# Two transformer-like blocks on one core: six gate slabs split in three passes and moved ahead, with the work around them reordered

## The chip, the cores and the metric

The kernel runs on 1 core of a Trainium2 chip. The metric is device time in microseconds (us) of one execution. TensorE (PE) multiplies, ScalarE (ACT) and VectorE (DVE) work elementwise, GpSimd (POOL) here only makes remainders of weights, and SyncE (SP) issues every transfer. A name such as `ps` is the one PSUM tensor of eight banks, which all engines but POOL read and write.

## The reference

The input is 256 tokens of width 1024. Two layers of `first_block` run, then one block of another kind. What matters is the first kind:

```
h = rms_norm(x, norm1_g);  z = h @ w_in
cq, ckv, kpe, gq, gk, gv, glr, gr, su, gates = split_in(z)
o_a = mla_mixer(cq, ckv, kpe, ...)        # low-rank attention, 8 heads
o_b = gla_mixer(gq, gk, gv, glr, gr, ...) # gated linear attention, chunks of 64
o_c = s5_mixer(su, lam_re, lam_im, ...)   # diagonal complex scan over time
g = sigmoid(gates + gate_b)               # 3 x 1024 gate columns
merged = g0*(o_a @ w_br_mla) + g1*(o_b @ w_br_gla) + g2*(o_c @ w_br_s5)
x = x + merged @ w_out
x = x + square(relu(rms_norm(x, norm2_g) @ w_ff1)) @ w_ff2
```

The last block projects queries, keys, values and gates, runs a dilated attention with a relative position bias, a convolution and its layer norm, a projection with a norm behind it, and a gated feed-forward part (tanh form of silu) with another norm behind it.

## The kernel before

Activations stand transposed, channels on partitions and the 256 tokens along the free axis. Weights come in slabs of 128x1024 numbers (512 KB), in the fixed order of `first_slabs`; a ring of three buffers holds raw slabs, and each split slab also has a rounded part `w_hi` (made by ACT) and a remainder `w_lo` (made by POOL from `raw` and `w_hi`). There are two ways to multiply by a slab. `product` uses the split form: three matmuls of type fp32r per 128 rows, 24 for a slab. `product32` uses the raw slab in full fp32: 8 matmuls for a slab, each of which the trace shows as two records. Before the change the 24 slabs of gate columns (`gates`) all use `product32` with the full-precision `hN`.

The order of each engine is written out by hand; counting semaphores hold it together, and nothing reorders it. In one layer TensorE does the 19 slabs of `Z`, four slabs of the values `gv`, then the small products for the S5 scan, four slabs `UQ`, two slabs `UKV`, and then a long stretch in which small products that depend on VectorE alternate with gate slabs. The names in this stretch are: `drive(h)` feeds step h of the S5 scan (its result is waited for as `bu_ps`), `outputs(h)` takes its states (`s_ok`); `head_sums` makes the squares' sums of q or k; `state_sums` makes the chunk states of the linear attention; `scores(n)` starts attention step n. VectorE's order there is: scale q (waits `qk_rs`, from ACT), `rotate_and_scan(2)` and `states(2)`, the masked copy into `Am` (raises `am_ok`), scale k, the running states `St` (raises `st_ok`), `rotate_and_scan(3)`, `y_take`, `states(3)`, the rotary parts of q in two halves, `rotate_and_scan(4)`, and the norm of the linear attention's output (raises `of_ok`, for which `scores(0)` waits). The decay of the scan (`lam_a`, `lam_s`) is computed at the head of a layer by some twenty tiny operations on VectorE and nine on ACT.

The diff touches `norm_rows`, `post_norm`, both feed-forward loops, `second_tables`, and the per-layer programs of ACT, DVE and PE.

Of the kernel before, what the change touches and what calls it, by code (L numbers as in the profile page):

```python
# [51 lines left out]
RING = 3  # L52

# [134 lines left out]
def build(nc, A, consts_dram, oneh_dram, where, out_dram, scratch):  # L188
# [21 lines left out]
    I_Z, I_GV, I_UQ, I_UKV, I_GATE = 0, 19, 23, 27, 29  # L210
# [18 lines left out]
    with ctx:  # L229
# [91 lines left out]
        Am = WK[:, 2560:3584].rearrange("p (h b c) -> p h b c", h=GH, b=NT)  # L321
        St = WK[:, 3584:4352].rearrange("p (n a e) -> p n a e", n=3, a=2)
# [3 lines left out]
        W4 = [[MD[:, 8192 + 512 * i:8704 + 512 * i].rearrange("p (j t) -> p j t", j=2) for i in range(4)],  # L326
# [96 lines left out]
        rot_ok = sig("rot_ok", 3)  # L423
        rot_rd = sig("rot_rd", 2)
# [101 lines left out]
        tab_z = sig("tab_z", 0)  # L526
# [30 lines left out]
        co_ok = sig("co_ok", 0)  # L557
        post_rs = sig("post_rs", 0)
# [34 lines left out]
        def norm_rows(act, A_, l, k, b, ready):  # L593
# [101 lines left out]
        def second_tables(sp):  # L695

            sp.dma_start(oneh, oneh_dram[:, 0:384]).then_inc(tab_in.s, 16)
            for g in range(3):
                sp.dma_start(tabl[33 * g:33 * g + 32, :], oneh_dram[33 * g:33 * g + 32, 384:408]).then_inc(tab_z.s, 16)
            for g in range(3):  # L700
                sp.dma_start(tabl[33 * g + 32:33 * g + 33, :], oneh_dram[33 * g + 32:33 * g + 33, 384:408])\
                    .then_inc(tab_in.s, 16)
            sp.dma_start(wdw, A["w_dw_2"][0]).then_inc(tab_in.s, 16)

        def second_bias(sp):

            for g in range(3):
                sp.dma_start(tabl[33 * g:33 * g + 32, 8 * g:8 * g + 8],
                             A["rel_bias_table_2"][:, 8 * g:8 * g + 8]).then_inc(tab_in.s, 16)
# [44 lines left out]
        def act_second(act):  # L754
# [47 lines left out]
            def post_norm(k, slab):  # L802

                act.preload_act_table_set("natural_log_exp_and_others")
                for b in range(NT):
                    if b == 0:
                        act.wait_ge(tm_out.s, tm_out(L, 3 * k - 1))
                    else:
                        act.wait_ge(used.s, used(L, slab + 1))
                    c = slice(16 + b, 17 + b)  # L810
                    link(A_(sqt[:, b, :], ps_half(k, b), ACT.Square, accum_out=nt[:, c]))
                    link(A_(nt[:, c], nt[:, c], ACT.Ln, scale=1.0 / DM, bias=C("eps4" if k == 1 else "eps")))
                    A_(nt[:, c], nt[:, c], ACT.Exp, scale=-0.5).then_inc(post_rs.s, 1)
                    if b == 0:
                        prep(slab + 3)
# [88 lines left out]
            for c in range(NC2):  # L904
                if c >= 2:
                    act.wait_ge(ff2_ok.s, c - 1)
                u = V_FF + 2 * c
                th, gt, up_ = ffb[c % 2]
                evacuate(u, up2_at(c) + 1, [(gt, pair(u % 3), ACT.Copy, {}),
                                            (th, pair(u % 3), ACT.Tanh, dict(scale=0.5))])  # L910
                evacuate(u + 1, up2_at(c) + 3, [(up_, pair((u + 1) % 3), ACT.Copy, {})])
# [3 lines left out]
        def dve_second(dve):  # L915
# [1512 lines left out]
```

## Time and profile before

| | before |
|---|---|
| median of 3 runs | 1540.09 us (1539.19 to 1540.39) |
| profiled execution, its own time | 1536.8 us |
| its span, first to last instruction | 1535.0 us |
| mean granted TensorE clock | 0.995 |
| busy: DVE, ACT, POOL | 58%, 45%, 58% of the span |
| split slabs of layers 1 and 2 (POOL L1283) | 206 |

The profile gives times of one execution. "Busy" of TensorE is counted with overlapping matmuls, so the cost of one is read from the distance between starts and not from its length. A row of the timeline is: start, length, engine, line, operation, output and inputs, shape, count; in brackets the idle time of that engine just before and who ended it. The first layer begins at 0, the second at about 505 us, the last block at about 1010 us.

### The profile page before, as it was taken

The numbers are of one execution on the slowest core, as the hardware profiler recorded it, in microseconds if no ns is written. First come the engines' busy times: TensorE is split into PE (matmuls) and PEld (weight loads), VectorE is DVE, ScalarE is ACT, GpSimd is POOL, SyncE is SP. The second block draws the span as 40 slices with busy tenths as digits, with TensorE's granted clock in tenths as the row PEclk, the third lists the DMA queues.
The fourth block names the chain that finished last, engine by engine and source line by source line (L and its number), as shares of the span: only waits on it lengthen the run. The fifth ranks groups of instructions, "written<-read, shape, count | busy, mean of one in ns | idle before, by whom it ended". The sixth has DMA issues, their size and how long they took to land.

```text
span 1535.0 us, 23998 instructions
## 1 busy us (share of the span) xinstructions
PE 1485.0 (97%) x9775; PEld 1317.3 (86%) x9775; DVE 889.6 (58%) x1407; ACT 698.4 (45%) x1052; POOL 882.8 (58%) x364
## 2 busy tenths in 40 slices
PE   7999999999999999999999999999999999899997
PEld 6977778889899897777788888989999988799996
DVE  5878875443433687886434455338993454265545
ACT  6544222554444654422255344464445655554443
POOL 4710000878888671000087788868885536688885
PEclk9999999999999999999999999999999999999999
DMA  6633344656666563333365577656664434456653
GB/s 187 162 107 78 96 106 123 193 153 188 183 185 187 150 174 87 94 96 100 124 194 162 173 218 218 190 152 186 180 188 124 135 104 124 137 177 183 190 179 124
DMA packets 321784, 234.47 MB, mean 153 GB/s; under 512 B 9676, under 2 KB 305131, under 8 KB 321674
## 3 DMA queue, kind: packets, MB, share of 16 engines
q1 hardware_dynamic: 321674, 232.94, 52.2%
q8 instruction: 77, 1.26, 0.4%
q14 instruction: 33, 0.27, 0.1%
HBM read 231.82 MB, written 1.09 MB: 152 GB/s over the span
## 4 chain that ended last, share of the span: by engine, by line
PE 84%; issue 5%; ACT 4%; POOL 4%; DVE 2%; DMA 1%; SPq 0%; POOLq 0%; DVEq 0%; ACTq 0%
PE ps L672 18%; PE ps L1943 14%; PE ps L1059 7%; PE ps L1060 7%; PE ps L1061 7%; PE ps L1926 6%; PE ps L1928 6%; PE ps L1927 6%; POOL w_lo L1283 4%; PE ps L1134 1%; PE ps L1171 1%; PE ps L2063 1%; PE ps L2077 1%; ACT w_hi L1317 1%; PE ps L2044 1%
## 5 line engine op out<-in xcount | busy, mean ns | idle before, releaser
L1283 POOL TENSOR_TENSOR w_lo<-raw,w_hi 128x1024 fp32r<-128x1024 f32 (+1 forms) x206 | 504.6, 2467 | 499.6 <-ACT w_hi L1317 497.2
L751 POOL TENSOR_TENSOR w_lo<-raw,w_hi 128x1024 fp32r<-128x1024 f32 x154 | 378.0, 2468 | 138.3 <-ACT w_hi L773 132.8
L1317 ACT ACTIVATE w_hi<-raw 128x1024 fp32r<-128x1024 f32 (+1 forms) x206 | 218.1, 1060 | 241.6 <-PE ps L672 75.8
L1059 PE MATMUL ps<-h_hi,w_hi 128*128 128x256 f32 x864 | 246.3, 285 | 1.8 <-DVE h_lo L928 1.3
L1060 PE MATMUL ps<-h_lo,w_hi 128*128 128x256 f32 x864 | 244.3, 283 | 0.0
L1061 PE MATMUL ps<-h_hi,w_lo 128*128 128x256 f32 x864 | 244.2, 283 | 0.0
L1926 PE MATMUL ps<-h_hi,w_hi 128*128 128x256 f32 (+1 forms) x816 | 233.3, 286 | 6.4 <-POOL w_lo L1283 4.3
L1927 PE MATMUL ps<-h_lo,w_hi 128*128 128x256 f32 (+1 forms) x816 | 231.3, 283 | 0.0
L1928 PE MATMUL ps<-h_hi,w_lo 128*128 128x256 f32 (+1 forms) x816 | 231.2, 283 | 0.0
L773 ACT ACTIVATE w_hi<-raw 128x1024 fp32r<-128x1024 f32 x154 | 162.0, 1059 | 116.2 <-PE ps L1061 43.3
L1943 PE MATMUL ps<-hN,raw 128*128 128x256 f32 x768 | 174.9, 383 | 0.0
L1059 PEld LDWEIGHTS ps<-h_hi,w_hi 128*128 128x128 f32 x864 | 165.5, 192 | 2.9 <-issue 2.4
L1943 PEld LDWEIGHTS ps<-hN,raw 128*128 128x128 f32 x768 | 143.0, 190 | 27.3 <-issue 9.1
L1060 PEld LDWEIGHTS ps<-h_lo,w_hi 128*128 128x128 f32 x864 | 165.6, 192 | 0.4
L1061 PEld LDWEIGHTS ps<-h_hi,w_lo 128*128 128x128 f32 x864 | 165.5, 192 | 0.0
L1926 PEld LDWEIGHTS ps<-h_hi,w_hi 128*128 128x128 f32 (+1 forms) x816 | 156.3, 192 | 9.9 <-POOL w_lo L1283 5.4
L1927 PEld LDWEIGHTS ps<-h_lo,w_hi 128*128 128x128 f32 (+1 forms) x816 | 156.5, 192 | 1.1
L1928 PEld LDWEIGHTS ps<-h_hi,w_lo 128*128 128x128 f32 (+1 forms) x816 | 156.4, 192 | 0.0
L1559 DVE TENSOR_TENSOR fr<-fr 128x512 f32<-128x512 f32 (+1 forms) x34 | 32.6, 960 | 199.6 <-ACT fr L1325 199.5
L672 PE MATMUL ps<-w_hi,c_hi 128*128 128x512 f32 x344 | 110.6, 400 | 5.3 <-POOL w_lo L1283 3.0
L672 PE MATMUL ps<-w_lo,c_hi 128*128 128x512 f32 x344 | 109.5, 396 | 0.0
L672 PE MATMUL ps<-w_hi,c_lo 128*128 128x512 f32 x344 | 109.5, 396 | 0.0
(325 smaller groups left out, 2523.6 us busy)
## 6 DMA issues: line engine op xcount, KB each, us to landing
raw<-in_w_in_dram SPq DMA_DIRECT2D x160, 512.0 KB, 3.8
raw<-in_w_ff_dram SPq DMA_DIRECT2D x128, 512.0 KB, 4.1
raw<-in_w_ffn_in_dram SPq DMA_DIRECT2D x44, 512.0 KB, 3.9
raw<-in_w_ffn_out_dram SPq DMA_DIRECT2D x22, 512.0 KB, 3.5
raw<-in_w_out_dram SPq DMA_DIRECT2D x16, 512.0 KB, 3.4
raw<-in_w_br_gla_dram SPq DMA_DIRECT2D x8, 512.0 KB, 3.5
raw<-in_w_br_mla_dram SPq DMA_DIRECT2D x8, 512.0 KB, 3.6
raw<-in_w_br_s_dram SPq DMA_DIRECT2D x8, 512.0 KB, 4.0
```

The source lines that it names most:

```text
L672: last = MM(out(2 * b + h), x[:, k, tb], y[:, 512 * h:512 * h + 512], start=first_k and n == 0, stop=last_k and n == 2, skip_group_check=True)
L751: nc.gpsimd.tensor_tensor(out=w_lo[(NS * L + i) % RING][:, 0:kt * n], in0=raw[(NS * L + i) % RING][:, 0:kt * n], in1=w_hi[(NS * L + i) % R ...
L773: A_(w_hi[(NS * L + i) % RING][:, 0:kt * n], raw[(NS * L + i) % RING][:, 0:kt * n], ACT.Copy).then_inc(hi_done.s, 1)
L1059: MM(out, w[0], x[0], start=first_k, stop=False, skip_group_check=skip)
L1060: MM(out, w[0], x[1], start=False, stop=False, skip_group_check=skip)
L1061: return MM(out, w[1], x[0], start=False, stop=last_k, skip_group_check=skip)
L1283: nc.gpsimd.tensor_tensor(out=w_lo[(NS * l + i) % RING][:, 0:kt * n], in0=raw[(NS * l + i) % RING][:, 0:kt * n], in1=w_hi[(NS * l + i) % R ...
L1317: A_(w_hi[(NS * l + i) % RING][:, 0:kt * n], raw[(NS * l + i) % RING][:, 0:kt * n], ACT.Copy)\
L1926: a = MM(out, w[0], x[0], start=first_k, stop=False, skip_group_check=skip)
L1927: MM(out, w[0], x[1], start=False, stop=False, skip_group_check=skip)
L1928: return MM(out, w[1], x[0], start=False, stop=last_k, skip_group_check=skip)
L1943: last = MM(out, w[:, k, c0:c0 + n], x[:, x0 + k, :], start=k == 0, stop=k == kt - 1)
```

## The change

The gate slabs 0 to 5 of each layer are now split slabs: they are multiplied by `product` with `h_hi` and `h_lo`, and stand in the slab order behind the four `gv` slabs, ahead of `UQ`. The S5 transposes of B stand behind `Z` slab 16, those of C and the product of `glr` behind `Z` slab 18, `drive(0)` behind two `gv` slabs, `drive(1)` between the early gate slabs, `outputs(0)` and `drive(2)` between the `UKV` slabs. The decay's VectorE part stands ahead of `norm_lo` in layer 1 and behind it in layer 2 (before: behind `norm_h` in both), and its ACT part ahead of the first evacuation of `Z`. Scratch memory changes place (`Am` and `St` to `MD`, one set of scan buffers to `WK`). The feed-forward products write their DVE intermediates into PSUM, the norm behind a projection multiplies by its weight first and in PSUM, the first norm row block is squared in one operation, and the bias tables of the last block come as one array in one transfer.

```diff
+GATES_Z = 6
...
+    gates = [(0, KD, C_GATE + P * gate_tile(i), P) for i in range(24)]
+    s += [("w_in_z", *g) for g in gates[:GATES_Z]]
     s += [("mla_w_uq", 0, 3, 2 * QK * i, 2 * QK) for i in range(4)]
     s += [("mla_w_ukv", 0, 2, 512 * i, 512) for i in range(2)]
-    s += [("w_in", 0, KD, C_GATE + P * gate_tile(i), P) for i in range(24)]
+    s += [("w_in", *g) for g in gates[GATES_Z:]]
...
+                        if i < GATES_Z:
+                            last = product(l, gate_slab(i), out, 0, P, h_hi, h_lo)
+                        else:
+                            last = product32(l, gate_slab(i), out, 0, P, hN)
...
+                if l == 0:
+                    decay()
                 norm_lo(dve, stt, l, col, "norm1_g")
+                if l:
+                    decay()
...
+                gates(0, 4)
+                pe.wait_ge(bu_rd.s, bu_rd(l, 1))
+                drive(1)
+                gates(4, 6)
                 for s in range(4):
                     i = I_UQ + s
...
                 head_sums(qsq, U_QS)
-                outputs(0)
-                gates(0, 2)
-                pe.wait_ge(bu_rd.s, bu_rd(l, 2))
-                drive(2)
+                gates(6, 8)
+                outputs(1)
                 pe.wait_ge(qkt_ok.s, qkt_ok(l, 1))
+                pe.wait_ge(kr_ok.s, kr_ok(l, 1))
...
                 last.then_inc(a_ps.s, 1)
-                gates(2, 4)
...
                 state_sums(2, PO, 256)
-                outputs(1)
                 pe.wait_ge(bu_rd.s, bu_rd(l, 3))
                 drive(3)
                 pe.wait_ge(am_ok.s, am_ok(l, 1))
                 state_sums(1, PA[2], 0).then_inc(ds_ps.s, 1)
-                gates(4, 6)
                 pe.wait_ge(st_ok.s, st_ok(l, 1))
...
                 rotate_q(0)
-                gates(6, 7)
+                gates(8, 9)
                 pe.wait_ge(rot_rd.s, rot_rd(l, 1))
                 rotate_q(1)
-                gates(7, 8)
...
-                    gates(8 + b, 9 + b)
-                gates(10, 11)
+                    gates(9 + b, 10 + b)
...
-                    link(tt(f, f, f, ALU.mult))
-                    link(V.tensor_copy(f_hi[c % 2][:, :, :], f))
-                    split_lo(f_lo[c % 2][:, :, :], f, f_hi[c % 2][:, :, :]).then_inc(ff_sq.s, 1)
+                    link(tt(x, fr[:, c % 2, :, :], x, ALU.mult))
+                    link(V.tensor_copy(f_hi[c % 2][:, :, :], x))
+                    split_lo(f_lo[c % 2][:, :, :], x, f_hi[c % 2][:, :, :]).then_inc(ff_sq.s, 1)
...
+            if b == 0:
+                act.wait_ge(*ready(1))
+                A_(sqt[:, 0, :], xt[:, 0, :], ACT.Square, accum_out=c[2]).then_inc(norm_sq.s, 2)
...
-            sp.dma_start(oneh, oneh_dram[:, 0:384]).then_inc(tab_in.s, 16)
-            for g in range(3):
-                sp.dma_start(tabl[33 * g:33 * g + 32, :], oneh_dram[33 * g:33 * g + 32, 384:408]).then_inc(tab_z.s, 16)
...
+            sp.dma_start(PT2[0][0:99, 0:408], A["bias_tables"]).then_inc(tab_in.s, 16)
...
-                link(stt(gt, th, 1.0, gt, ALU.add, ALU.mult))
-                link(tt(gt, gt, up_, ALU.mult))
+                link(stt(gt, th, 1.0, gate, ALU.add, ALU.mult))
+                dve.wait_ge(used.s, used(L, up2_at(c) + 4))
+                link(tt(up_, gt, up_, ALU.mult))
```

First place, TensorE in the middle of a layer. Before, from the third step of the scan's drive to the linear attention's output (`L1943` are gate slabs, eight matmuls each; `L2063` is `drive`, `L2077` `outputs`, `L2044` `head_sums`, `L2156` `state_sums`, `L2175` the output that waits for `st_ok`):

```order
L2063 MATMUL ps<-Z,BT 128x256 x4
L2137 MATMUL ps<-cst,WK 128x128 x4
L2044 MATMUL ps<-G,cst 96x512 x4
L2146 MATMUL ps<-WK 128x128 x8
L1943 MATMUL ps<-hN,raw 128x256 x16
L2156 MATMUL ps<-gv,WK 64x128 x8
L2077 MATMUL ps<-Z,CT 32x256 x4
L2063 MATMUL ps<-Z,BT 128x256 x4
L2156 MATMUL ps<-gv,WK 64x128 x4
L1943 MATMUL ps<-hN,raw 128x256 x16
L2175 MATMUL ps<-WK,gv 128x128 x2
```

Two pairs of gate slabs stand in this stretch, and one more directly ahead of it, behind the head sums of q. The same place now, from the head sums of q on (`L1965` gate slabs, `L2034` `drive`, `L2121` `outputs`, `L2106` `head_sums`, `L2188` `state_sums`, `L2205` the output that waits for `st_ok`):

```order
L2106 MATMUL ps<-MD,cst 96x512 x4
L1965 MATMUL ps<-hN,raw 128x256 x16
L2121 MATMUL ps<-Z,CT 32x256 x4
L2170 MATMUL ps<-cst,WK 128x128 x4
L2106 MATMUL ps<-G,cst 96x512 x4
L2179 MATMUL ps<-WK 128x128 x8
L2188 MATMUL ps<-gv,WK 64x128 x8
L2034 MATMUL ps<-Z,BT 128x256 x4
L2188 MATMUL ps<-gv,WK 64x128 x4
L2205 MATMUL ps<-MD,gv 128x128 x2
```

One pair of gate slabs is left between the head sums of q and the linear attention's output, where three pairs stood; no gate slab stands behind the head sums of k any more.

Second place, VectorE at the head of the first layer. Before (`L1562` is `norm_lo`, `L616` `norm_h`, the rest the decay):

```order
L1562 SCALAR_TENSOR_TENSOR h_lo<-ps,cols,h_hi 128x256 x8
L616 TENSOR_SCALAR hN<-ps,cols 128x256 x8
L1597 TENSOR_SCALAR sms<-cols 128x16
L1559 TENSOR_TENSOR ps<-sms,ps 128x16
L1559 TENSOR_TENSOR ps<-cols,ps 128x16
L1600 TENSOR_SCALAR ps<-ps 128x16
L1601 CAST smi<-ps 128x16
L1602 CAST sms<-smi 128x16
```

And now:

```order
L1611 TENSOR_SCALAR sms<-cols 128x16
L1576 TENSOR_TENSOR ps<-sms,ps 128x16
L1576 TENSOR_TENSOR ps<-cols,ps 128x16
L1614 TENSOR_SCALAR ps<-ps 128x16
L1615 CAST smi<-ps 128x16
L1616 CAST sms<-smi 128x16
L1579 SCALAR_TENSOR_TENSOR ps<-sms,ps 128x16 x3
L1619 TENSOR_SCALAR ps<-ps 128x16
L1579 SCALAR_TENSOR_TENSOR h_lo<-ps,cols,h_hi 128x256 x8
```

The decay's first part stands ahead of `h_lo`, for which the first slab's matmuls wait.

Third place, ACT at the head of a layer. Before (`L1335` is `h_hi`, `L1317` a slab's `w_hi`, `L1325` an evacuation of `Z`, the rest the decay):

```order
L1335 ACTIVATE h_hi<-ps,cols 128x256 x8
L1317 ACTIVATE w_hi<-raw 128x1024 x2
L1325 ACTIVATE Z<-ps 128x512
L1317 ACTIVATE w_hi<-raw 128x1024 x2
L1325 ACTIVATE Z<-ps 128x512
L1368 ACTIVATE sms<-ps 128x16
```

And now:

```order
L1350 ACTIVATE h_hi<-ps,cols 128x256 x8
L1332 ACTIVATE w_hi<-raw 128x1024
L1370 ACTIVATE sms<-ps 128x16
L1371 ACTIVATE ps<-ps 128x16
L1372 ACTIVATE ps<-sms 128x16
L1374 ACTIVATE sms<-cols 128x16
```

The decay on ACT stands three slabs earlier: `w_hi` of slabs 3 to 5 is made behind it instead of ahead of it.

## Rows read from the trace of the kernel before

**Rows 1.** The page's part 1: busy time, share and instructions.

```profile
PE 1485.0 (97%) x9775; PEld 1317.3 (86%) x9775; DVE 889.6 (58%) x1407; ACT 698.4 (45%) x1052; POOL 882.8 (58%) x364
```

**Rows 2.** The page's part 4: shares of the chain that ended last.

```profile
PE 84%; issue 5%; ACT 4%; POOL 4%; DVE 2%; DMA 1%; SPq 0%; POOLq 0%; DVEq 0%; ACTq 0%
```

**Rows 3.** Timeline of PE, 24 matmuls of a split slab apart.

```profile
26.82 0.28 PE L1926 MATMUL ps<-h_hi,w_hi 128*128 128x256 f32 x1
...
29.70 0.28 PE L1926 MATMUL ps<-h_hi,w_hi 128*128 128x256 f32 x1
```

**Rows 4.** Timeline of PE, middle of the first layer.

```profile
118.70 3.82 PE L2044 MATMUL ps<-MD,cst 96*96 96x512 f32 x8
...
123.44 7.17 PE L1943 MATMUL ps<-hN,raw 128*128 128x256 f32 x32
130.54 1.14 PE L2063 MATMUL ps<-Z,BT 32*128 32x256 f32 x8
...
185.64 0.71 PE L2222 MATMUL ps<-MD 96*128 96x128 f32 x4
```

**Rows 5.** Timeline of ACT, the exponential that releases q's scaling.

```profile
123.28 1.91 ACT L1446 ACTIVATE MD<-MD 96x2048 f32<-96x2048 f32 x1
```

**Rows 6.** Timeline of DVE, the same stretch of the first layer.

```profile
125.22 2.35 DVE L1562 SCALAR_TENSOR_TENSOR MD<-MD,cols 96x2048 f32<-96x2048 f32 x1 [0.86 <-ACT MD L1446]
131.80 2.48 DVE L1559 TENSOR_TENSOR MD<-ps,AR 128x512 f32<-128x512 f32 x4 [4.23 <-PE ps L2063]
...
141.98 1.33 DVE L1762 COPY_PREDICATED WK<-cst,ps 128x512 f32<-128x512 int32 x2
...
149.61 2.48 DVE L1559 TENSOR_TENSOR Z<-ps,AR 128x512 f32<-128x512 f32 x4
...
161.01 1.22 DVE L1559 TENSOR_TENSOR MD<-ps,cst 32x1024 f32<-32x1024 f32 x1 [0.75 <-PE ps L2187]
...
166.50 1.22 DVE L1559 TENSOR_TENSOR MD<-ps,cst 32x1024 f32<-32x1024 f32 x1 [1.76 <-PE ps L2187]
...
180.04 1.22 DVE L1562 SCALAR_TENSOR_TENSOR MD<-sq,MD 128x1024 f32<-128x1024 f32 x1
...
186.46 0.43 DVE L1559 TENSOR_TENSOR ps<-ps,cst 128x256 f32<-128x256 f32 x1 [0.94 <-PE ps L2222]
```

**Rows 7.** Timeline of PE, the wait in the first slabs of each layer.

```profile
36.68 0.48 PE L1926 MATMUL ps<-h_hi,w_hi 128*128 128x256 f32 x1 [2.13 <-POOL w_lo L1283]
...
532.95 0.39 PE L1926 MATMUL ps<-h_hi,w_hi 128*128 128x256 f32 x1 [2.13 <-POOL w_lo L1283]
```

**Rows 8.** Table of stretches: PE, PEld, DVE, ACT, POOL busy, clock, DMA.

```profile
36.00:42.00 6.00, 5.32 (x32) 5.32 (x33) 5.32 (x18) 1.16 (x2) 5.29 (x3) 0.72 0.58 152
```

**Rows 9.** Timelines of POOL, DVE and ACT at the heads of the layers.

```profile
15.10 2.37 POOL L1283 TENSOR_TENSOR w_lo<-raw,w_hi 128x1024 fp32r<-128x1024 f32 x1 [2.28 <-ACT w_hi L1317]
...
24.69 2.40 POOL L1283 TENSOR_TENSOR w_lo<-raw,w_hi 128x1024 fp32r<-128x1024 f32 x1 [0.80 <-ACT w_hi L1317]
...
24.80 2.31 DVE L1602 CAST sms<-smi 128x16 f32<-128x16 int32 x1
...
515.26 4.80 POOL L1283 TENSOR_TENSOR w_lo<-raw,w_hi 128x1024 fp32r<-128x1024 f32 x2 [1.51 <-ACT w_hi L1317]
...
525.59 0.18 ACT L1368 ACTIVATE sms<-ps 128x16 f32<-128x16 f32 x1
...
528.11 1.28 ACT L1378 ACT_TABLE_LOAD   x1
```

**Rows 10.** Timelines of PE and DVE: transfers' wait, last block's end.

```profile
859.76 1.22 PE L672 MATMUL ps<-w_hi,c_hi 128*128 128x512 f32 x2 [2.53 <-POOL w_lo L1283]
...
1522.04 0.74 PE L672 MATMUL ps<-w_hi,c_hi 128*128 128x512 f32 x2 [2.30 <-DVE c_lo L928]
...
1529.67 0.76 DVE L928 SCALAR_TENSOR_TENSOR ps<-ps,nt,Up 128x512 f32<-128x512 f32 x1
...
1531.86 0.69 DVE L925 TENSOR_TENSOR xt<-xt,ps 128x512 f32<-128x512 f32 x1
```

More of the change, by code:

```diff
@@ L804, in post_norm @@
                 act.preload_act_table_set("natural_log_exp_and_others")
+                n = 4 * (k - 1)
                 for b in range(NT):
[L806 to L813, printed above, removed]
+                    rs_, part = nt[:, 16 + b:17 + b], nt[:, 18 + b:19 + b]
+                    for i in (2 * b, 2 * b + 1):
+                        if i < 3:
+                            act.wait_ge(tm_out.s, tm_out(L, 3 * (k - 1) + i + 1))
+                        else:
+                            act.wait_ge(used.s, used(L, slab + 1))
+                        y = ps_out(i) if k == 1 else ps_tok(i)
+                        A_(tok(sqt, i), y, ACT.Square, accum_out=rs_ if i % 2 else part).then_inc(post_sq.s, 1)
+                        if i % 2 == 0:
+                            act.wait_ge(post_sq.s, n + i + 1)
+                            link(A_(part, part, ACT.Identity, scale=1.0 / DM, bias=C("eps4" if k == 1 else "eps")))
+                    act.wait_ge(post_sq.s, n + 2 * b + 2)
+                    link(A_(rs_, rs_, ACT.Ln, scale=1.0 / DM, bias=part))
+                    A_(rs_, rs_, ACT.Exp, scale=-0.5).then_inc(post_rs.s, 1)
                     if b == 0:
@@ L907, in act_second @@
                 u = V_FF + 2 * c
[L908 to L911, printed above, removed]
+                th = ffb[c % 2][0]
+                evacuate(u, up2_at(c) + 1, [(th, pair(u % 3), ACT.Tanh, dict(scale=0.5))])
+                prep(up2_at(c) + 3 + RING)
             prep(N2)
@@ L1423, in _ @@
                 A_(e1[:, :, :], e1[:, :, :], ACT.Ln, bias=C("one")).then_inc(gg_ex.s, 1)
-                for u in range(4):
-                    b = pair((U_UQ + u) % PGF)[0:QK]
-                    evacuate(U_UQ + u, I_UQ + u, [
-                        (q[0:QK, 2 * u:2 * u + 2, :], b, ACT.Copy, {}),
-                        (qsq[0:QK, 2 * u:2 * u + 2, :], b, ACT.Square, {})])
+                take_gv(1)
+                gate(0)
                 act.wait_ge(cs_ok.s, cs_ok(l, 1))
@@ L1437, in _ @@
                     .then_inc(ge_ok.s, 1)
+                gate(1)
+                gate(2)
+                for u in range(4):
+                    b = pair((U_UQ + u) % PGF)[0:QK]
+                    evacuate(U_UQ + u, I_UQ + u, [
+                        (q[0:QK, 2 * u:2 * u + 2, :], b, ACT.Copy, {}),
+                        (qsq[0:QK, 2 * u:2 * u + 2, :], b, ACT.Square, {})])
                 def head_rms(k, dst, U):
@@ L2001, in _, with drive @@
                 x_to_h(pe, l, 0, 1)
+                def drive(h):
+                    g, j0 = h // 2, 2 * (h % 2)
+                    for jj in range(2):
+                        rr_ = slice(32 * (j0 + jj), 32 * (j0 + jj) + 32)
+                        for r in range(2):
+                            last = MM(pair(4 + jj)[:, r, :], BT[rr_, r, g, :], Z[rr_, Z_SU + g, :],
+                                      start=True, stop=True)
+                    last.then_inc(bu_ps.s, 1)
                 pe.wait_ge(consts_all.s, 16)
```

273 lines of the change are left out of this document (140 added, 133 removed).

## The prediction

> **What bounds the kernel now.** I read the page's busy table first: TensorE is busy 97% of the span and VectorE 58% [rows 1]. The chain that ended last runs 84% through TensorE [rows 2]. So a microsecond taken from TensorE's own work is won, a microsecond in which it waits is lost, and VectorE and POOL count only where one of them arrives last. Shares of the whole span hide the one thing that matters for this change: in the middle of each layer there is a stretch in which VectorE is nearly full. I read it next, in the timelines of TensorE and VectorE. Call T the end of the head sums of q, at 118.70 + 3.82 = 122.5 [rows 4]. From there TensorE reaches `scores(0)` at 185.6, that is T+63.1 [rows 4]. VectorE finishes what `scores(0)` waits for at 180.04 + 1.22 = 181.3, T+58.7 [rows 6]. In between it idles only 4.23, 0.75 and 1.76, each time for TensorE, 6.7 in all; its 0.86 ahead of the scaling of q is for ACT's exponential, which ends at 125.19 [rows 5, 6]. TensorE therefore is not waiting in this stretch, but only because gate slabs fill it. Last I read the waits: 2.13 early in each layer [rows 7], and 2.53 and 2.30 in the last block [rows 10].
>
> **The slabs' price.** A split slab takes from 26.82 to 29.70, 2.88 us [rows 3]. An unsplit pair takes from 123.44 to 130.54, 7.10, so 3.55 for one [rows 4]. Twelve slabs change form: 12 x 0.67 = -8.0 us. ACT makes twelve more `w_hi` and POOL twelve more `w_lo` of some 2.4 us each [rows 9]; POOL is at 58% and idle where they fall, so I cost these at nothing; without that cover they are the second rival.
>
> **The gap in the middle of a layer.** This is the term that decides. Six gate slabs, three pairs, leave the part behind T and lie ahead of it now: 3 x 7.10 = 21.3 less work for TensorE behind T. It takes one `outputs` and one `drive` off it as well, of eight records each, 1.0 and 1.1 by the row of 1.14 [rows 4]. Together 23.4, so TensorE's own work from T to `scores(0)` falls from 63.1 to 39.7. All that VectorE has to do from T stays, in the same order: scale q, step 2 of the scan, the copy to `Am`, scale k, the running states, step 3, the rotary halves, step 4, the norm of the output. That queue is 58.7 long with its 6.7 of idle, and 52.0 without. `drive(2)` being early removes the 4.23, and I take all three as removed. The second rotary half can't be: TensorE sends `rotate_q(1)` only when VectorE has read the first, for which I leave 0.7. So `scores(0)` starts at T+52.7, and TensorE idles 52.7 - 39.7 = about 13; I take 12.9. By the trace, 23.4 is taken away, 4.4 of it was slack of TensorE over VectorE and 6.7 of VectorE over TensorE, and the rest must show as waits. They spread: the first at the state sums for `am_ok` (the copy at 141.98 follows scan step 2 [rows 6]), the larger at `st_ok`, which has the scaling of k and the running states ahead of it, and the last at `outputs(2)` and `scores(0)` for `of_ok`. Behind the waiting matmul stands TensorE's whole queue, among it the products that VectorE needs next, so the wait can't be used for other slabs. Bounds: nothing lost (0), if VectorE had 13 us more in reserve than its idle rows show; 16.7 lost, if its idle stays for lack of anything sent early. I stay at 12.9, near which the rows of idle time are.
>
> **What is late next.** Behind `scores(0)` VectorE still has the second part of step 4, from 181.3 to 185.5 (it next idles 0.94 up to 186.46) [rows 6]. Before, this lay beside the 4.4 of slack. Now it stands ahead of the first softmax, and TensorE has a gate slab of 3.55 to cover 4.3 plus the first softmax row: I take +1.5, between 0 and 4.3. Small things in the same layers: waits for B and for the transposed values go, a bank is freed later by the evacuation of `gv`, and the remainders of the early gate slabs come only a few tenths ahead; I net these at -0.4, between -1.5 and +2.
>
> Per layer 12.9 + 1.5 - 0.4 = 14.0; two layers +28.0, with the slabs' price +20.0.
>
> **Heads of the layers.** In layer 1 the wait of 2.13 at 36.68 goes, because ACT's decay no longer stands ahead of a `w_hi`, and with it the lower clock behind it: the stretch 36 to 42 has 0.72 granted [rows 7, 8], which I price at 1.5. Against that, nine operations stand ahead of `h_lo` on VectorE. By the rows they are short, but the copy of 16 columns `sms<-smi` lasted 2.31, from 24.80 to 27.11, while POOL worked from 24.69 to 27.09 [rows 9]: it ended when POOL's operation ended. At its new place POOL's operation of 15.10 to 17.47 covers it [rows 9], so I give the first slab 2.2 of delay. Net -1.4; bounds -3.6 and +1. The Trainium skill ("SBUF — State Buffer", Who interferes with whom) says that VectorE and GpSimd share one port pair as an exclusive lock, held for a whole instruction by whoever started first; a cast is among the operations that can want it. The trace agrees with its 2.31; without that rule one would give the small operations some 0.2 each and the net would be -3.0.
>
> In layer 2 the decay stands behind `norm_lo` and ahead of the full-precision `hN`. Its first operations meet POOL's two remainders, 515.26 to 520.06, of which the first ends at 517.7 [rows 9]. `lam_a` then comes at about 519.7, ACT's decay lasts 2.5 (525.59 to 528.11) [rows 9], the next `w_hi` is ready at 523.3 and its remainder 2.4 later at 525.7. TensorE wants that slab at about 522.0: a wait of 3.7, less the 2.13 at 532.95 [rows 7], +1.6. Bounds -2 and +4.
>
> **The last block.** The bias tables come in one transfer in place of several; the wait of 2.53 at 859.76 for a remainder whose slab queued behind them goes [rows 10], with about 1.2 of slower clock behind it: -3.7, between 0 and -4. The feed-forward's last `c_lo` no longer waits behind VectorE's copies with two inputs in SBUF: -2.3 of 1522.04 [rows 10]. At the very end four pairs of 0.76 and 0.69 [rows 10] stand between the last norm and the output; the multiply by the weight now lies ahead of the norm's scale, so that less of each pair stands behind it: -1.9, two thirds of the four 0.76, between 0 and -3. Other norms of this kind -0.5. Squaring the first row block in one operation begins later but is shorter, +0.1 at each of four norms: +0.5. Together -4.2, and with the transfers -7.9.
>
> **Sum.** +20.0 - 1.4 + 1.6 - 7.9 = +12.3. The profiled execution took 1536.8, of which the span is 1535.0; it becomes 1549.1. The median of the runs is 1540.09, 3.3 above the profiled one, 0.2%: a difference of executions that the change does not touch. So 1552.4.
>
> **Rivals.** *The stretch does not bind.* If VectorE catches up, what is left is the slabs' price, the small items, the heads and the last block: -8.0 - 0.8 + 0.2 - 7.9 = -16.5, 1523.6. It needs `of_ok` at T+40 in place of T+52. For it speaks that VectorE gets 21 us of TensorE's work ahead of T in which to run ahead; against it, that the scaling of q stands first in its queue behind T and ACT's exponential releases that only at T+2.7 [rows 5], and that the 52 is time in which it was working. It decides from 12 us of VectorE's queue done ahead of T; the new order moves only the drive of step 2, not the step. Chance 0.08.
>
> *The remainders fall behind as well.* In the ten slabs from the first of `gv` to gate slab 5, TensorE uses one each 2.88 while POOL needs 2.4, and in the same time VectorE runs multiplies with both inputs in SBUF, of 1.2 and more, as the 1.22 in the output's norm [rows 6]. If each of these takes a turn with POOL, a slab costs 2.4 + 1.2 = 3.6 and six slabs lose 0.7 each, 4 per layer, and a lower clock behind the waits some more: +21 to +26 in all, 1561 to 1566. For it speaks the copy of 2.31; against it, that at 58% POOL holds its pace in the `Z` slabs, with no wait but 2.13. Chance 0.13. By the same rule of the Trainium skill (same page and section) every VectorE operation with two SBUF inputs contends with a POOL operation that reads SBUF, which would make this the rule and not the exception; no row here shows six of them in such a run.
>
> *Half of it hides.* If VectorE's operations are shorter in the new stretch, because POOL has less to do beside them, a layer loses 7 in place of 14: 1538, no change. Chance 0.07.
>
> **How the numbers follow.** Forecast 0.72, rivals 0.08, 0.13 and 0.07. The forecast's own spread is 2 per layer in the gap and some 3 in the rest: 1546 to 1559. For 8 in 10 I take 1544 to 1560, which takes in part of the port's case; fast and half-hidden cases stay outside. Within 0.2% means 3.1 us, about what a measurement can tell. Faster: 0.08 and a little of the third case, 0.09. Same: 0.05. Slower: 0.86.
>
> **What would show it.** Right: in each layer TensorE idles some 13 us between T and `scores(0)`, released by VectorE (`Am`, `St`, output norm), and VectorE has no idle time above 1 us there except for ACT's exponential. The early gate slabs start 2.88 apart. The waits of 2.53 and 2.30 are gone; in layer 2 a remainder of an early `Z` slab is late by 3 to 4. Wrong: the waits at the state sums are under 3 us together (then T's own position hides something that I missed), or gate slabs 0 to 5 start 3.5 apart (then POOL is the bound), or the granted clock falls for long after the new gaps.

## The result, and the profile after

| | before | changed |
|---|---|---|
| median | 1540.24 us (1539.19 to 1540.39) | 1554.87 us (1552.25 to 1559.43) |
| ratio | | 1.0100, 95% interval 1.0075 to 1.0124 |
| span of the profiled execution | 1535.0 us | 1553.1 us |
| mean granted clock | 0.995 | 0.984 |

The change makes the kernel 1.0% slower, 14.6 us by the medians; 1552.4 was forecast. The two profiled spans are 18.1 apart, because the profiled execution of before (1536.8) lay 3.4 under its median and that of the changed kernel on its own. The page's part 1 of the changed kernel, to be held against [rows 1]:

```profile
PE 1485.6 (96%) x9871; PEld 1323.3 (85%) x9871; DVE 759.8 (49%) x1407; ACT 696.5 (45%) x1036; POOL 893.6 (58%) x376
```

TensorE's busy time is the same although 12 slabs became shorter, and VectorE has 130 us less of busy time while the kernel is slower. The chain of waits shows what took TensorE's place (part 4, against [rows 2]):

```profile
PE 80%; DVE 7%; issue 4%; ACT 4%; POOL 3%; DMA 1%; SPq 0%; DVEq 0%; POOLq 0%; ACTq 0%
```

VectorE had 2% of the chain and has 7%. The timeline of TensorE shows where, in the first layer; T, the end of q's head sums, is 135.35 + 3.82 = 139.2 here (against [rows 4]):

```profile
135.35 3.82 PE L2106 MATMUL ps<-MD,cst 96*96 96x512 f32 x8
139.12 7.14 PE L1965 MATMUL ps<-hN,raw 128*128 128x256 f32 x32
...
155.90 0.65 PE L2188 MATMUL ps<-gv,WK 64*64 64x128 f32 x8 [1.29 <-DVE MD L1784]
162.28 1.22 PE L2205 MATMUL ps<-MD,gv 128*128 128x128 f32 x4 [5.73 <-DVE MD L1579]
...
179.84 1.14 PE L2034 MATMUL ps<-Z,BT 32*128 32x256 f32 x8 [0.26 <-DVE MD L1576]
...
192.84 0.68 PE L2250 MATMUL ps<-MD 96*128 96x128 f32 x4 [1.65 <-DVE MD L1579]
```

`scores(0)` starts at T+53.7, where T+63.1 was before. In between TensorE waits four times, 8.9 us in all, each time for VectorE. The remaining 44.7 are still 5.0 more than the 39.7 of work. The table of stretches shows where (columns as in [rows 8]):

```profile
156.00:162.00 6.00, 0.55 (x8) 0.31 (x8) 5.85 (x7) 1.74 (x2) 0.00 (x0) 0.70 0.00 0
162.00:170.00 8.00, 7.72 (x40) 6.47 (x40) 7.89 (x14) 0.00 (x0) 0.00 (x0) 0.50 0.00 0
170.00:174.00 4.00, 4.00 (x21) 1.80 (x20) 3.65 (x6) 1.02 (x1) 0.00 (x0) 0.74 0.00 0
```

TensorE worked 0.55 of the 6 us up to 162, and the clock granted from 162 to 170 is 0.50, the 1.2 GHz level. The products behind the wait ran at half speed: from the first of them to the first gate slab behind them it is 10.7 us (162.28 to 172.97), where before it was 6.2 (154.66 to 160.90). That is 4.5 of the 5.0. VectorE meanwhile is 5.85 of 6.00 and 7.89 of 8.00 busy. Its timeline, against [rows 6]:

```profile
141.94 2.35 DVE L1579 SCALAR_TENSOR_TENSOR MD<-MD,cols 96x2048 f32<-96x2048 f32 x1 [15.01 <-ACT MD L1466]
144.32 2.48 DVE L1576 TENSOR_TENSOR WK<-ps,AR 128x512 f32<-128x512 f32 x4
...
154.51 1.33 DVE L1784 COPY_PREDICATED MD<-cst,ps 128x512 f32<-128x512 int32 x2
...
162.14 2.48 DVE L1576 TENSOR_TENSOR Z<-ps,AR 128x512 f32<-128x512 f32 x4
...
173.07 1.22 DVE L1576 TENSOR_TENSOR MD<-ps,cst 32x1024 f32<-32x1024 f32 x1 [0.28 <-PE ps L2217]
...
178.56 1.22 DVE L1576 TENSOR_TENSOR MD<-ps,cst 32x1024 f32<-32x1024 f32 x1 [1.76 <-PE ps L2217]
...
191.47 1.23 DVE L1579 SCALAR_TENSOR_TENSOR MD<-sq,MD 128x1024 f32<-128x1024 f32 x1
```

The idle 4.23 is gone, 0.75 became 0.28, 1.76 stayed, and VectorE ends this queue at 192.7, T+53.5. Ahead of the scaling of q VectorE sits idle for 15.0 us: that is what the six slabs bought, idle time for the engine that is late behind T. In layer 2 the same waits stand at the same distances (1.28, 5.73, 0.26, 1.65).

The distance between the two kernels, by the start of the same operation in both, splits the total:

| up to | before | changed | distance | this part | forecast |
|---|---|---|---|---|---|
| T, layer 1 | 122.5 | 139.2 | +16.7 | +16.7 | +18.0 |
| `scores(0)`, layer 1 | 185.6 | 192.8 | +7.2 | -9.5 | -10.4 |
| second norm, layer 1 | 323.0 | 332.6 | +9.6 | +2.4 | +1.1 |
| second norm, layer 2 | 817.2 | 839.9 | +22.7 | +13.1 | +11.6 |
| last block's first slab | 1014.7 | 1036.3 | +21.6 | -1.1 | -3.7 |
| end | 1535.0 | 1553.1 | +18.1 | -3.5 | -4.2 |

(The +18.0 is six slabs of 2.88 and the 2.1 of one `outputs` and one `drive`, less 1.4 at the head; -10.4 is T+52.7 less T+63.1.) The stretch with the bias table is off by most, 2.6; layer 2 comes next with 1.5. Of a single row not more than some 1.5 us can be read: up to the product `ps<-sq,cst` behind the first twelve slabs of layer 1, the changed kernel took 54.8 us, and the run with the decay moved in layer 2 (below), which has the same code there, took 56.1.

The places of the smaller terms in the changed kernel, TensorE's timeline, against [rows 7] and [rows 10]:

```profile
18.78 0.55 PE L1948 MATMUL ps<-h_hi,w_hi 128*128 128x256 f32 x1 [3.63 <-DVE h_lo L1579]
...
93.14 0.28 PE L1948 MATMUL ps<-h_hi,w_hi 128*128 128x256 f32 x1
...
96.02 0.28 PE L1948 MATMUL ps<-h_hi,w_hi 128*128 128x256 f32 x1
...
289.90 0.35 PE L1948 MATMUL ps<-o_hi,w_hi 128*128 128x256 f32 x1 [2.21 <-POOL w_lo L1298]
...
535.27 0.58 PE L1948 MATMUL ps<-h_hi,w_hi 128*128 128x256 f32 x1 [3.43 <-POOL w_lo L1298]
...
881.94 1.17 PE L688 MATMUL ps<-w_hi,c_hi 128*128 128x512 f32 x2 [2.00 <-POOL w_lo L1298]
```

The two rows at 93 and 96 are the first products of two early gate slabs, 2.88 apart. The cast that [rows 9] have at 2.31 is here, in layer 1 and in layer 2:

```profile
14.86 2.14 DVE L1616 CAST sms<-smi 128x16 f32<-128x16 int32 x1
...
528.22 0.17 DVE L1616 CAST sms<-smi 128x16 f32<-128x16 int32 x1
```

And two stretches of the table (columns as in [rows 8]), the one behind the wait of 3.43 and the one ahead of the wait of 2.00:

```profile
535.00:541.00 6.00, 5.73 (x28) 5.73 (x29) 5.34 (x14) 0.36 (x2) 4.90 (x3) 0.53 0.69 176
...
879.40:881.00 1.60, 0.54 (x3) 0.10 (x1) 1.01 (x2) 1.43 (x3) 1.48 (x1) 1.00 0.07 20
```

In the second, the DMA engines are busy for 0.07 on average, which is about one of sixteen, and move 20 GB/s.

### The profile page after: what moved, and what is told of

Read it like the earlier page. It is cut to its first block, busy times and chain, and to the rows that moved or that the text cites. A ratio compares the mean times of both kernels' runs of the same rounds, so it can differ in the third digit from the quotient of the medians.

```text
span 1553.1 us, 24229 instructions
## 1 busy us (share of the span) xinstructions
PE 1485.6 (96%) x9871; PEld 1323.3 (85%) x9871; DVE 759.8 (49%) x1407; ACT 696.5 (45%) x1036; POOL 893.6 (58%) x376
## 3 DMA queue, kind: packets, MB, share of 16 engines
q8 instruction: 78, 1.28, 0.3%
## 4 chain that ended last, share of the span: by engine, by line
PE 80%; DVE 7%; issue 4%; ACT 4%; POOL 3%; DMA 1%; SPq 0%; DVEq 0%; POOLq 0%; ACTq 0%
PE ps L688 17%; PE ps L1965 10%; PE ps L1948 7%; PE ps L1949 7%; PE ps L1950 7%; PE ps L1074 6%; PE ps L1075 6%; PE ps L1076 6%; POOL w_lo L1298 2%; DVE WK L1576 2%; PE ps L1149 1%; DVE MD L1579 1%; PE ps L1186 1%; DMA raw<-in_w_ff_dram 1%; ACT w_hi L1332 1%
## 5 line engine op out<-in xcount | busy, mean ns | idle before, releaser
L1298 POOL TENSOR_TENSOR w_lo<-raw,w_hi 128x1024 fp32r<-128x1024 f32 x218 | 521.7, 2404 | 503.8 <-ACT w_hi L1332 502.7
L756 POOL TENSOR_TENSOR w_lo<-raw,w_hi 128x1024 fp32r<-128x1024 f32 x154 | 371.6, 2421 | 144.8 <-ACT w_hi L778 143.4
L1332 ACT ACTIVATE w_hi<-raw 128x1024 fp32r<-128x1024 f32 x218 | 230.1, 1058 | 242.5 <-PE ps L688 91.3
L1948 PE MATMUL ps<-h_hi,w_hi 128*128 128x256 f32 (+1 forms) x912 | 261.9, 287 | 9.2 <-DVE h_lo L1579 5.7
L1949 PE MATMUL ps<-h_lo,w_hi 128*128 128x256 f32 (+1 forms) x912 | 259.4, 284 | 0.0
L1950 PE MATMUL ps<-h_hi,w_lo 128*128 128x256 f32 (+1 forms) x912 | 259.3, 284 | 0.0
L778 ACT ACTIVATE w_hi<-raw 128x1024 fp32r<-128x1024 f32 x154 | 161.7, 1057 | 142.0 <-PE ps L1076 76.0
L1948 PEld LDWEIGHTS ps<-h_hi,w_hi 128*128 128x128 f32 (+1 forms) x912 | 175.9, 193 | 13.0 <-issue 7.7
L1949 PEld LDWEIGHTS ps<-h_lo,w_hi 128*128 128x128 f32 (+1 forms) x912 | 176.0, 193 | 1.2
L1576 DVE TENSOR_TENSOR ps<-fr,ps 128x512 f32<-128x512 f32 (+1 forms) x36 | 24.0, 666 | 269.5 <-ACT fr L1340 258.0
L1965 PE MATMUL ps<-hN,raw 128*128 128x256 f32 x576 | 131.8, 383 | 0.0
L1965 PEld LDWEIGHTS ps<-hN,raw 128*128 128x128 f32 x576 | 107.0, 190 | 21.1 <-issue 7.7
```

Source lines behind the costliest of these rows:

```text
L756: nc.gpsimd.tensor_tensor(out=w_lo[(NS * L + i) % RING][:, 0:kt * n], in0=raw[(NS * L + i) % RING][:, 0:kt * n], in1=w_hi[(NS * L + i) % R ...
L778: A_(w_hi[(NS * L + i) % RING][:, 0:kt * n], raw[(NS * L + i) % RING][:, 0:kt * n], ACT.Copy).then_inc(hi_done.s, 1)
L1298: nc.gpsimd.tensor_tensor(out=w_lo[(NS * l + i) % RING][:, 0:kt * n], in0=raw[(NS * l + i) % RING][:, 0:kt * n], in1=w_hi[(NS * l + i) % R ...
L1332: A_(w_hi[(NS * l + i) % RING][:, 0:kt * n], raw[(NS * l + i) % RING][:, 0:kt * n], ACT.Copy)\
L1948: a = MM(out, w[0], x[0], start=first_k, stop=False, skip_group_check=skip)
L1949: MM(out, w[0], x[1], start=False, stop=False, skip_group_check=skip)
```

## The experiments

The kernel before ran beside each group, with medians of 1537.9, 1538.4 and 1538.8. Differences against the changed kernel are taken between the ratios, times 1540. Its own ratio is known to 0.0025, which is 3.8 us, so a smaller difference rests on the traces and not on the medians. T and `scores(0)` come from each run's timeline.

### Is the gap VectorE's queue?

Put gate work back behind T. `GATES_Z` becomes 4, and the two pairs stand unsplit behind T; the run with 2 puts three pairs there.

```diff
-GATES_Z = 6
+GATES_Z = 4
...
-                gates(4, 6)
                 for s in range(4):
                     i = I_UQ + s
...
                 head_sums(qsq, U_QS)
-                gates(6, 8)
+                gates(4, 6)
...
                 state_sums(1, PA[2], 0).then_inc(ds_ps.s, 1)
+                gates(6, 8)
                 pe.wait_ge(st_ok.s, st_ok(l, 1))
```

> Four gate slabs early in place of six: the pair 4,5 is unsplit again and stands behind the head sums of q, and the pair 6,7 stands ahead of the wait for the running states, where the kernel before had a pair. Theory (VectorE's queue behind T sets the start of scores(0), T being the end of q's head sums): scores(0) stays at T+53.6, T comes 2 x 2.88 = 5.8 earlier, the wait for St (5.73) goes to nearly nothing; -5.8 per layer, -11.5 in all, 1543. Rival (the gap is not VectorE's queue; a slab put there only adds its own time): the two unsplit slabs cost 0.67 more each, +2.7, 1557.5.

Measured: 1542.56, ratio 1.0026 (1.0011 to 1.0040), 11.4 under the changed kernel. T is 133.8 and `scores(0)` 185.91, T+52.1. TensorE's timeline:

```profile
150.52 0.65 PE L2187 MATMUL ps<-gv,WK 64*64 64x128 f32 x8 [1.28 <-DVE MD L1784]
...
185.91 0.95 PE L2250 MATMUL ps<-MD 96*128 96x128 f32 x4 [1.65 <-DVE MD L1579]
```

The wait of 5.73 is gone, and 7.1 us of work was put behind T while `scores(0)` even came a little earlier relative to T. The rival's +2.7 is out.

> Two gate slabs early in place of six: pairs 2,3, 4,5 and 6,7 stand unsplit at the three places of the kernel before; everything else of the change stays. Theory: TensorE's work between T and scores(0) is 39.7 + 14.2 = 53.9, equal to VectorE's 53.6, T comes 4 x 2.88 = 11.5 earlier, scores(0) at T+54 to T+56; -10 to -11.5 per layer, -21 in all, 1534, below the kernel before. Rival as in the run with four: +5.3, 1560.

Measured: 1537.53, ratio 0.9994 (0.9984 to 1.0004), 16.3 under the changed kernel and equal to before. T is 128.1, and `scores(0)` comes at T+56.2:

```profile
184.29 0.68 PE L2251 MATMUL ps<-MD 96*128 96x128 f32 x4 [1.64 <-DVE MD L1579]
```

The first pair put back gave 11.4 and the second only 4.9: TensorE's own 53.9 (39.7 and two pairs of 7.1) is nearly VectorE's time now. The size, -21, was too large, by 2.3 per layer of T+56.2 over T+53.9.

### Is it the length of the queue or the order of its operands?

Step 2 of the scan goes into the 15.0 us of idle time.

```diff
                 tt(kpe_r[NOPE:QK], kpe_r[NOPE:QK], kpe_g[NOPE:QK], ALU.add).then_inc(kr_ok.s, 1)
+                rotate_and_scan(2)
+                states(2)
...
                 dve.wait_ge(qk_n.s, qk_n(l, 2))
-                rotate_and_scan(2)
-                states(2)
```

> VectorE does step 2 of the scan (10.2 us) ahead of the scaling of q, in its idle time of 15.0 us. Theory A (every operation behind T waits for its own releaser, and the copy to Am and k's scaling wait for TensorE's products and for ACT): VectorE then idles for the A matrix (T+13.4) and for k's factors (T+15), St comes 1.4 earlier; -1.4 to -2 per layer, 1551 to 1552. Theory B (only the length of VectorE's queue counts): -9 per layer, 1537.

Measured: 1553.26, ratio 1.0095 (1.0080 to 1.0110), 0.8 under the changed kernel, with an interval that holds no difference. Theory B, -9 per layer, is out. Theory A fits the trace: T is 139.8 and `scores(0)` starts at 191.7, T+51.8, 1.8 earlier than in the changed kernel; the medians do not confirm its size. VectorE's timeline shows 8.3 of the 10.2 us come back as idle time:

```profile
142.61 2.35 DVE L1579 SCALAR_TENSOR_TENSOR MD<-MD,cols 96x2048 f32<-96x2048 f32 x1 [0.41 <-ACT MD L1466]
153.24 1.36 DVE L1783 COPY_PREDICATED MD<-cst,ps 128x512 f32<-128x512 int32 x2 [8.28 <-PE ps L2178]
```

The matrix A stands on TensorE behind a gate pair and k's head sums. The next run takes the pair away from there.

```diff
                 head_sums(qsq, U_QS)
-                gates(6, 8)
                 outputs(1)
...
                 drive(3)
+                gates(6, 8)
                 pe.wait_ge(am_ok.s, am_ok(l, 1))
                 state_sums(1, PA[2], 0).then_inc(ds_ps.s, 1)
```

> As the run with step 2 early, and TensorE does k's head sums, the A matrix, two state sums and drive(3) ahead of gate pair 6,7 instead of behind it. Theory A: VectorE's operands now come at T+6 and T+9, its queue ends at T+45 to T+47 in place of T+53.6, the wait for St goes; -6 to -8 per layer, -14 in all, 1541. Theory B: as the run before, 1537. If neither the operands nor the queue bind: 1551 to 1555.

Measured: 1546.13, ratio 1.0055 (1.0036 to 1.0073), 6.9 under the changed kernel, half of what was expected. VectorE's timeline names the other half:

```profile
147.09 1.35 DVE L1783 COPY_PREDICATED MD<-cst,ps 128x512 f32<-128x512 int32 x2 [1.76 <-PE ps L2177]
...
156.87 0.42 DVE L1795 COPY MD<-ps 128x256 f32<-128x256 f32 x1 [3.58 <-PE ps L2186]
...
175.85 1.22 DVE L1576 TENSOR_TENSOR MD<-ps,cst 32x1024 f32<-32x1024 f32 x1 [2.79 <-PE ps L2216]
```

I had put the pair ahead of the last state sum, for which `St` waits 3.58. `scores(0)` starts at T+49.9, where T+45 to T+47 was expected. Neither theory gave the size: queue length and operand order bind together.

### The smaller terms

The slab's price: the early slabs unsplit, in the same order.

```diff
-    s += [("w_in_z", *g) for g in gates[:GATES_Z]]
+    s += [("w_in", *g) for g in gates[:GATES_Z]]
...
-                            last = product(l, gate_slab(i), out, 0, P, h_hi, h_lo)
+                            last = product32(l, gate_slab(i), out, 0, P, hN)
```

> The six early gate slabs stay where the change put them but are multiplied unsplit (hN and the raw slab). Theory (a slab's price is 3.55 against 2.88, and POOL's and ACT's work for the split is hidden): T comes 6 x 0.67 = 4.0 later in each layer, nothing else moves, +8.0, 1563. Rival (the remainders of the early slabs hold TensorE or VectorE back, through the port that POOL and VectorE share): less than +4, under 1559.

Measured: 1561.39, ratio 1.0149 (1.0129 to 1.0169), 7.5 above the changed kernel. T comes 3.5 later, and the waits for VectorE behind it are the same 1.29, 5.73 and 1.64. The price of -8.0 fits, within the intervals of some 4 us, and the trace shows no wait up to `scores(0)` that the split adds.

The bias table: only the convolution's weights are moved.

```diff
             sp.dma_start(PT2[0][0:99, 0:408], A["bias_tables"]).then_inc(tab_in.s, 16)
-            sp.dma_start(wdw, A["w_dw_2"][0]).then_inc(tab_in.s, 16)
...
+                    if i == I_FF + 14 and l == DEPTH - 1:
+                        sp.dma_start(wdw, A["w_dw_2"][0]).then_inc(tab_in.s, 16)
```

> The transfer of the convolution's weights (31 rows of 4 KB, 124 KB) is issued two slabs later than the bias table instead of directly behind it. Theory (this transfer, which the change left alone, keeps a single DMA engine busy at 20 GB/s for some 6 us, and the raw slab queued behind it is what comes late): the wait of 2.0 for a remainder moves to the later slab or shrinks, the raw slab behind the bias table lands in under 5 us; total between -3 and 0, 1552 to 1555. Rival (the bias table's own transfer does it): the wait of 2.0 stays at its place.

Measured: 1553.58, ratio 1.0101 (1.0084 to 1.0117), no difference. But the wait moved with the transfer:

```profile
887.38 0.39 PE L1949 MATMUL ps<-h_hi,w_hi 128*128 128x256 f32 x1 [2.38 <-POOL w_lo L1299]
```

Two slabs later, about the same size, and no wait is left at the old place: at either place it is the transfer of 31 rows of 4 KB that delays the raw slab behind it, and the bias table's does not. In the changed kernel, the stretch of 20 GB/s ahead of the wait (0.07 of the DMA engines busy) fits one transfer that keeps about one engine. The kernel before issued the same transfer at the same place.

The feed-forward products back in SBUF (the diff is the part of the change on `f`, `gt` and `up_`, reversed).

```diff
-                    x = pair((U_FF + c) % PGF)
+                    f = fr[:, c % 2, :, :]
...
-                    link(tt(x, fr[:, c % 2, :, :], x, ALU.mult))
+                    link(tt(f, f, f, ALU.mult))
...
-                link(stt(gt, th, 1.0, gate, ALU.add, ALU.mult))
+                link(stt(gt, th, 1.0, gt, ALU.add, ALU.mult))
```

> The feed-forward products of all three blocks keep their VectorE operands in SBUF as in the kernel before, with the copies by ACT in the last block; norms, tables and the layers' middle as changed. Theory: the wait of about 2.3 ahead of the last down projection comes back and VectorE's busy time grows by 110 to 130 us, since its operations with two operands in SBUF run to the end of POOL's; +2.3, 1557. Rival (the last block's gain of 4.3 comes from the norm at the end alone): +0.

Measured: 1557.43, ratio 1.0121 (1.0104 to 1.0138), 3.2 above the changed kernel, with intervals that overlap. What is sure is the trace: TensorE's timeline has the wait of [rows 10] again:

```profile
1542.70 1.22 PE L688 MATMUL ps<-w_hi,c_hi 128*128 128x512 f32 x2 [2.31 <-DVE c_lo L940]
```

VectorE's busy time is 919.4 in place of 759.8. Its groups by line (count, busy us, mean ns of one), first of this run, then of the changed kernel, show one operation with both inputs in SBUF and with one:

```profile
L1572 DVE TENSOR_TENSOR c_lo<-fr,c_hi 128x512 fp32r<-128x512 f32 x32 | 88.9, 2777 | 1.1
```

```profile
L1576 DVE TENSOR_TENSOR c_lo<-ps,c_hi 128x512 fp32r<-128x512 f32 x32 | 22.1, 691 | 1.1
```

The last `c_lo` of this run, at 1541.96, took 0.69 as well, although both of its inputs lie in SBUF: POOL's last remainder had ended at 1541.64. So the longer time comes with POOL's work beside it.

The decay ahead of `norm_lo` in both layers.

```diff
-                if l == 0:
-                    decay()
+                decay()
                 norm_lo(dve, stt, l, col, "norm1_g")
-                if l:
-                    decay()
```

> In layer 2 the decay on VectorE stands ahead of norm_lo, as in layer 1. Theory: the wait of 3.43 at the head of layer 2 goes, and the first slab starts 2 us later; -1 to -2, 1553. Rival (the decay's small operations are cheap beside h_lo at that place): the first slab starts under 1 us later, -3, 1552; other rival: they cost more than the wait, +1.

Measured: 1552.33, ratio 1.0094 (1.0078 to 1.0110), 0.9 under the changed kernel, not clear of no difference. The trace shows the exchange. From the second norm of layer 1 to the first slab of layer 2 it is 192.6 in place of 190.3, 2.3 more, so the first rival (under 1) is out. The wait of 3.43 behind is gone, and the first twelve slabs take 36.1 in place of 40.8, 4.7 less; that speaks against the second rival (the move costs more than the wait):

```profile
334.28 2.05 PE L652 MATMUL ps<-rs,xt 128*128 128x128 f32 x16 [1.44 <-ACT rs L625]
...
526.86 0.55 PE L1945 MATMUL ps<-h_hi,w_hi 128*128 128x256 f32 x1 [3.21 <-DVE h_lo L1579]
```

### A version that beats both

Four slabs early, step 2 of the scan in the idle time, all operands of VectorE first and the fillers behind them:

```diff
                 head_sums(qsq, U_QS)
-                gates(6, 8)
                 outputs(1)
...
                 state_sums(1, PA[2], 0).then_inc(ds_ps.s, 1)
+                gates(4, 6)
                 pe.wait_ge(st_ok.s, st_ok(l, 1))
...
                 rotate_q(0)
-                gates(8, 9)
+                gates(6, 7)
                 pe.wait_ge(rot_rd.s, rot_rd(l, 1))
                 rotate_q(1)
+                gates(7, 8)
...
-                    gates(9 + b, 10 + b)
+                    gates(8 + b, 9 + b)
+                gates(10, 11)
```

> A version built from the runs so far: four gate slabs early, step 2 of the scan ahead of the scaling of q, TensorE does k's head sums, the A matrix and all state sums directly behind q's head sums, gate pair 4,5 ahead of the wait for St, slabs 6 to 10 one by one behind it. Theory (both queues are counted with their operands): TensorE's work from T to scores(0) is 46.8 and VectorE's end is at T+45 to T+50, so the wait at scores(0) shrinks; T + 5.8 later than with two slabs early; 3 per layer under that run, 1532 on the scale on which the kernel before has 1538. Rival (the operands come late again at other places, as in the run with k's head sums first): scores(0) at T+51 or later, 1538 or more.

Measured: 1530.35, ratio 0.9946 (0.9932 to 0.9960). T is 134.7 and `scores(0)` follows at T+48.5 with no wait ahead of it. Two short waits are left on the way, 0.48 and 0.89:

```profile
183.18 0.71 PE L2248 MATMUL ps<-MD 96*128 96x128 f32 x4
```

The last run adds the decay's place and splits the convolution's weights:

```diff
+                    if i in (I_FF + 12, I_FF + 14, I_FF + 16, I_FF + 18) and l == DEPTH - 1:
+                        r0 = 4 * (i - I_FF - 12)
+                        r1 = min(r0 + 8, CONVW)
+                        sp.dma_start(wdw[r0:r1, :], A["w_dw_2"][0][r0:r1, :]).then_inc(tab_in.s, 16)
```

> The run before with two more edits: the decay ahead of norm_lo in both layers, and the convolution's weights in four transfers of 8 rows, one for every second slab. Theory: the wait of 3.4 in layer 2 goes for 2.3 at the first slab, the wait of 2 behind the bias table goes since no transfer holds one DMA engine for 6 us; -1 to -3 against the run before, 1530. Rival (four transfers hold the one engine as long in all and each delays a slab): no gain, or the wait shows up several times.

Measured: 1527.55, ratio 0.9920 (0.9906 to 0.9935), 0.8% under the kernel before. The wait of 2 behind the table is gone; the intervals of the last two runs just meet at 0.9935 and 0.9932, so the last step of 0.26% is likely and not proved, and its two edits are not told apart.

## Why the prediction was right, and where not

**The gap in the middle of a layer: right.** Forecast was `scores(0)` at T+52.7; it came at T+53.7. TensorE lost 13.9 against 39.7 of work, where 12.9 was taken. So the rival in which half of it hides (7 per layer) is out too. The form was half right: I had the loss as 13 of waits, and it is 8.9 of waits and 5.0 of slower matmuls, nearly all at the 1.2 GHz level behind the longest wait. A granted clock that falls behind the gaps stands in the prediction as a sign of being wrong, and it came. As I read it, the sum does not change by it, since VectorE is 5.85 of 6.00 and 7.89 of 8.00 us busy there and sets the end of the stretch; no run tested this apart. Nor did VectorE's idle time go as taken: I left 0.7 and 2.04 stayed (0.28 and 1.76), where the prediction's sign was nothing above 1 us. The upper bound of 16.7 was worked out wrongly: with all idle time kept, VectorE ends at T+58.7, and less 39.7 that is 19.0. That VectorE's queue is what binds, the run with four early slabs shows from the other side: 7.1 more work behind T, and 11.4 faster in two layers, where 11.5 was expected.

**Where the waits stand: right.** `am_ok` 1.3, `st_ok` 5.7, `of_ok` 1.65 (and 0.26 at a `drive`). At `outputs(2)` the timeline shows none; slow matmuls filled that time.

**What is late next: right in kind, too small.** Behind `scores(0)` a wait of 1.03 came in layer 1, and the remainders of the branch slabs cost 2.21 at 289.90 where 1.07 had been. The part is +2.4 against +1.1. What makes the remainders later there was not tested; some of it is scatter, since the run with the decay moved in layer 2 has the same code there and a wait of 1.11. Without the split it is 0.42.

**The slabs' price: right.** -8.0, and 7.5 by the run without the split. The rival that POOL falls behind in the early slabs is refuted: they start 2.88 apart (93.14 and 96.02), not 3.6, with no wait for a remainder among them, and TensorE's waits behind T are the same with and without the six remainders.

**Heads of the layers: the waits right, the clock behind them left out.** In layer 1 the wait of 2.13 at 36.68 went, and the cast of 16 columns took 2.14 at its new place, against the 2.31 it was priced by. In layer 2, with POOL idle from 527.30 on, the same cast took 0.17, and the wait is 3.43, forecast 3.7. The time from the first slab to the product behind the twelfth shows what was missing. In layer 2 it is 37.1 before and 40.8 now, +3.8 where +1.6 was forecast: the granted clock is 0.53 in the 6 us behind the wait. All nine kernels here with the decay at this place show a wait of 3.4 to 3.5 and took 38.4 to 40.9 for this part. In layer 1 the first slab starts 1.9 later and the part is 2.6 shorter, so -0.7 where -1.4 was forecast. I had priced the lower clock behind the wait that goes (1.5), and none behind the waits that come. Together the heads cost +3.0 where +0.2 was taken, so this term was mis-sized too.

**The transfers: wrong in size and in cause.** The step that failed most reads "the bias tables come in one transfer in place of several; the wait of 2.53 at 859.76 for a remainder whose slab queued behind them goes": -3.7. Measured is a wait of 2.00, still there, and -1.1 for the whole stretch. The cause I named was the wrong transfer. The row shows only that a remainder was late; which DMA stood ahead of its slab I took from the diff, and the convolution's weights, which no diff line touches, stood there as well. The moved transfer took the wait with it.

**The last block: right.** -3.5 against -4.2; the run with the products in SBUF has the wait of 2.31 at the old place, and 3.2 more in all, which by itself is not clear of nothing.

**The rival of no binding queue** (1523.6) failed where the prediction said it would: VectorE did get 15.0 us ahead of T, and stood idle in them. It asked for VectorE to be done when TensorE's own work is, T+40 with six early slabs. No run had this. With four early slabs, step 2 and the operands moved, it was met at that kernel's longer 46.8: VectorE ended at T+44.1, and the kernel reached 1530.

**What was luck.** The forecast is 2.5 from the median, and the cause and the size of the largest term bear that out. The sum of the terms, +12.3, is nearer to the medians' +14.6 than to the profiles' +18.1, because the profiled execution of before ran 3.4 under its median. Apart from T, every part of the table came out above its forecast, by 0.7 to 2.6.

## What to carry to other kernels

Work that keeps one engine busy while another catches up is not idle filler: before moving it, measure from a fixed point how long each engine's queue is without its idle rows, and move only the difference. Price the lower clock behind each wait that the change makes, and not only behind those that it takes away. Put what the late engine reads first and the filler behind it; a shorter queue alone gave 0.8 us, the same with its operands early 6.9. When a wait ends with a transfer, look at every transfer issued ahead of the late one, above all those that the change leaves alone.

## What the runs showed of the hardware

- A transfer of 31 rows of 4 KB cost TensorE a wait of 2.0 to 2.4 at either of the two places tried, and in the changed kernel the DMA engines moved 20 GB/s ahead of that wait, with 0.07 of them busy. In four parts (three of 8 rows, one of 7), one for every second slab, it cost none there; whether the size or the spacing does it was not told apart.
- 160 us less busy time of VectorE (759.8 against 919.4) came from placing operands in PSUM: one `c_lo` took 0.69 in place of 2.78. TensorE had waited for it at one place only, for 2.31, and 3.2 us of run time, not clear of nothing, is all that it was worth. The Trainium skill ("SBUF — State Buffer", Who interferes with whom) says that a VectorE operation with at most one input in SBUF, outside the modes that use two ports, does not contend with GpSimd. The 0.69 agrees, and so does the same 0.69 with both inputs in SBUF once POOL had finished.
- After 6 us in which TensorE worked 0.55, the granted clock was 0.50 for the next 8 us; after a first wait of 1.3 alone, in the run with four early slabs, it was 0.72 in the 6 us from 150 to 156. After the wait of 3.43 at the head of layer 2 it was 0.53 for 6 us, and twelve slabs with that wait took 40.8 us, where twelve slabs of 2.88 and the wait make 38.0. How much of this a shorter wait would save was not measured apart.
